# A two-block transformer kernel: mid-kernel loads issued by GpSimd, latent keys at 288 columns, memory squares added by VectorE, head sums in three steps

## What is computed

```python
kv_a = hk @ w_kv_a                                  # 1024 x (256 + 32)
c_kv, k_rope = jnp.split(kv_a, [KV_LORA_RANK], axis=-1)
mem_n = rms_norm_2(mem, mem_norm[l])                # needs the mean of mem * mem
o = rms_norm_2(o, subln) * (1.0 - lam_init)         # differential heads, 128 channels each
y_br = y_br * silu(gate);  y = concat(y_br, y_mem * silu(g_mem)) @ w_out
```

## Time and profile before

| | |
|---|---|
| median of 3 runs | 1167.52 us (1166.16 to 1168.13) |
| the profiled execution, its own time | 1172.58 us |
| its span, first to last instruction | 1170.7 us |
| mean granted TensorE clock | 0.979 of full speed |
| PE busy | 1122.1 us, 96% of the span |
| DVE, ACT, POOL busy | 470.7, 284.9, 53.7 us |
| DMA | 195.67 MB, mean 167 GB/s |

### The profile page before, as it was taken

One profiled execution on the slowest core, in us unless ns is written; L12 is line 12 of the kernel. 1 busy time (PEld: TensorE's weight loads), 2 busy tenths in 40 slices (PEclk: granted clock), 3 DMA queues, 4 the chain that ended last, 5 costly groups with the idle time before them and its releaser, 6 DMA issues.

```text
span 1170.7 us, 19356 instructions
## 1 busy us (share of the span) xinstructions
PE 1122.1 (96%) x8435; PEld 945.8 (81%) x8435; DVE 470.7 (40%) x947; ACT 284.9 (24%) x680; POOL 53.7 (5%) x70
## 2 busy tenths in 40 slices
PE   6888999999999999899999999999999999999997
PEld 4657888888887858588888888888899888887676
DVE  8886445434314518713000000234834541602621
ACT  4622510000002444612000000133303241202632
POOL 3110011111100000000000000000003000000000
PEclk7998999999999999999999999999999999999999
DMA  9985879999843344073544532453440003544220
GB/s 285 341 278 188 287 267 373 335 352 361 317 149 116 108 126 146 14 238 109 180 143 146 178 108 81 143 157 118 126 145 4 4 3 108 180 149 139 73 72 36
DMA packets 122019, 195.67 MB, mean 167 GB/s; under 512 B 5796, under 2 KB 104782, under 8 KB 115534
## 3 DMA queue, kind: packets, MB, share of 16 engines
q1 hardware_dynamic: 110778, 131.15, 35.0%
q0 software_dynamic: 9360, 59.77, 13.2%
q10 hardware_dynamic: 1796, 3.50, 1.0%
HBM read 191.53 MB, written 1.05 MB: 164 GB/s over the span
## 4 chain that ended last, share of the span: by engine, by line
PE 83%; DVE 10%; ACT 3%; issue 1%; DMA 1%; SPq 0%; ACTq 0%; DVEq 0%
PE psum L658 63%; PE psum L1029 13%; DVE arena L1717 3%; ACT arena L2562 2%; PE psum L933 2%; PE psum L1504 1%; DVE sq L1717 1%; DVE arena L1723 1%; DMA arena<-in_x 1%; ACT sq L2562 1%; DVE xT L1723 1%; PE psum L1479 1%; DVE arena L1981 1%; DVE arena L1720 1%; PE psum L1626 1%
## 5 line engine op out<-in xcount | busy, mean ns | idle before, releaser
L658 PE MATMUL psum<-hT,ring 128*128 128x256 f32 x1392 | 311.4, 381 | 1.7 <-DVE hT L1723 0.8
L658 PEld LDWEIGHTS psum<-hT,ring 128*128 128x128 f32 x1392 | 263.1, 191 | 41.0 <-issue 6.0
L2562 ACT ACTIVATE arena<-psum 128x256 f32<-128x256 f32 (+5 forms) x219 | 98.0, 475 | 649.1 <-PE psum L658 597.6
L658 PE MATMUL psum<-hT,arena 128*128 128x256 f32 (+1 forms) x960 | 165.2, 346 | 3.4 <-DVE hT L1717 3.4
L658 PEld LDWEIGHTS psum<-hT,arena 128*128 128x128 f32 (+1 forms) x960 | 143.9, 186 | 22.6 <-issue 4.5
L1717 DVE TENSOR_TENSOR arena<-arena,psum 128x256 f32<-128x256 f32 (+2 forms) x76 | 39.2, 530 | 264.2 <-ACT arena L2562 235.6
L658 PE MATMUL psum<-arena 64*64 64x64 f32 (+6 forms) x2156 | 108.0, 240 | 0.9 <-ACT arena L2562 0.5
L658 PEld LDWEIGHTS psum<-arena 64*64 64x64 f32 (+3 forms) x2156 | 91.0, 141 | 12.4 <-issue 8.6
L1029 PE MATMUL psum<-arena,ring 128*128 128x256 f32 x384 | 85.1, 380 | 0.0
L1029 PEld LDWEIGHTS psum<-arena,ring 128*128 128x128 f32 x384 | 72.6, 190 | 11.0 <-issue 1.2
L658 PE MATMUL psum<-ring,arena 128*128 128x256 f32 (+2 forms) x288 | 73.2, 415 | 0.5 <-ACT arena L2562 0.5
(11 more groups left out here) (259 smaller groups left out, 1112.8 us busy)
## 6 DMA issues: line engine op xcount, KB each, us to landing
aring<-in_ada_w POOLq DMA_DIRECT2D x36, 1024.0 KB, 8.5
ring<-in_a_w_in SPq DMA_DIRECT2D x14, 1024.0 KB, 5.4
arena<-in_ffn_w_gate SPq DMA_DIRECT2D x12, 1024.0 KB, 7.5
arena<-in_ffn_w_up SPq DMA_DIRECT2D x12, 1024.0 KB, 8.0
ring<-in_ffn_w_down SPq DMA_DIRECT2D x12, 1024.0 KB, 5.0
ring<-in_ffn_w_gate SPq DMA_DIRECT2D x10, 1024.0 KB, 9.4
ring<-in_ffn_w_up SPq DMA_DIRECT2D x10, 1024.0 KB, 7.6
arena<-in_ffn_w_down SPq DMA_DIRECT2D x10, 1024.0 KB, 5.0
```

The costliest lines, as they stand in the source:

```text
L658: return eng.matmul(dst, w, x, start=first, stop=last)
L2562: return eng.activation(dst, x, f, **k)
```

## The change

Five edits, none of which changes what is computed:

1. The 12 loads leave ACT's list and go to POOL's, each behind a wait for a point at which its destination is free: `("dn", 0, 3)` emptied, `q1_mean`, `("dn", 1, 3)` emptied, and `post_added`.
2. `w_kv_a` is split by rows (7 and 1 chunks k) instead of by columns; PE makes one pass of 288 columns.
3. The memory squares are taken by ACT in four pieces and added by DVE (`sum_squares`, behind `ada_bias(7)`); PE makes one matmul with ones, between `cqt` b = 0 and b = 1. ACT's root of it moves from ahead of part 4 to ahead of part 5.
4. RWKV: `scale_tokens(0, i)` goes into the last chunk, `memory_gate(0)` ahead of the last gain.
5. Last layer: head sums at u = 2, 3, 4 (four matmuls each); DVE copies the bank to SBUF at u = 4 and ACT takes the root of the copy; SiLU at 7, 8, 8; `gate_heads` ahead of memory step 11.

The diff, its core (indents shortened):

```diff
 pair_sum = stat[:, :].rearrange("p (m t) -> p m t", t=T)[:, 0:4:3, :]
 square_sum = stat[:, 0:T]
 root_cols, rstd_cols = stat[:, T:T + 2], stat[:, T + 4:T + 6]
-SUMS = [("ms", 1), ("ms", 2), ("ms", 3), ("ms", 4), ("ms_out", 0), ("ms", 5)]
+SUMS = [("ms", 1), ("ms", 2), "ms_mem", ("ms", 3), ("ms", 4), ("ms_out", 0), ("ms", 5)]
 COLUMN_NORMS = [("ms", 1), ("ms", 2), ("ms_out", 0)]
...
-SUM_STEP, SCALE_STEP, ROW_STEP = 4, 9, 10
-SILU_STEPS = [7, 8, 9]
+SUM_STEPS, SCALE_STEP, ROW_STEP = [2, 3, 4], 9, 10
+SILU_STEPS = [7, 8, 8]
...
 in_columns(("glu",), a["s5_w_glu"][0], D)
 swiglu_weights(0)
 w_kva = a["w_kv_a"].rearrange("(k p) n -> p k n", p=P)
-weights.append((w_kva[:, :, 0:RKV], (KC, RKV), ("kva", 1)))
-weights.append((w_kva[:, :, RKV:], (KC, DR), ("kva", 1)))
+KVA_SPLIT = KC - 1
+for ks in (slice(0, KVA_SPLIT), slice(KVA_SPLIT, KC)):
+    weights.append((w_kva[:, ks, :], (ks.stop - ks.start, RKV + DR), ("kva", 1)))
 weights.append((a["mla_w_dq"][0].rearrange("(k p) n -> p k n", p=P), (KC, RQ), ("cqt", 1)))
...
@@ -961,18 +962,9 @@
-    def mean_square(key, chunks, src, sig, count, pool="a"):
+    def mean_of_sum(key, pool="a"):
         eng.wait_ge(*next_bank(key, pool))
-        ps = bank_of(key)
-        for k in range(chunks):
-            eng.wait_ge(done(sig), count(k))
-            last = mm(ps[:, 0:T], ones, src[:, k, :], k == 0, k == chunks - 1)
-        last.then_inc(*fills(key))
-
-    def mean_of_sum(key):
-
-        eng.wait_ge(*next_bank(key))
         eng.wait_ge(done("square_sums"), SUMS.index(key) + 1)
         mm(bank_of(key)[:, 0:T], ones, square_sum).then_inc(*fills(key))
@@ -1153,26 +1145,24 @@
...
     ada_rows(7, "b")
     for b in range(2):
         eng.wait_ge(*next_bank(("kva", b)))
-    w, landed = panel()
-    eng.wait_ge(*landed)
+    kva_w = [panel() for _ in range(2)]
+    eng.wait_ge(*kva_w[0][1])
     for b in range(2):
         ps = bank_of(("kva", b))
         for k in range(KC):
             if b == 0:
                 eng.wait_ge(done("h_ready"), KC + k + 1)
-            mm(ps[:, 0:RKV], hT3[:, k, b * P:(b + 1) * P], w[:, k, :], k == 0, k == KC - 1)
+                if k == KVA_SPLIT:
+                    eng.wait_ge(*kva_w[1][1])
+            w = kva_w[0][0][:, k, :] if k < KVA_SPLIT else kva_w[1][0][:, k - KVA_SPLIT, :]
+            last = mm(ps[:, 0:RKV + DR], hT3[:, k, b * P:(b + 1) * P], w, k == 0, k == KC - 1)
+        last.then_inc(*fills(("kva", b)))
+    row_columns(7, row_late, "b")
     w, landed = panel()
     eng.wait_ge(*landed)
     for b in range(2):
-        ps = bank_of(("kva", b))
-        for k in range(KC):
-            last = mm(ps[:, RKV:RKV + DR], hT3[:, k, b * P:(b + 1) * P], w[:, k, :], k == 0, k == KC - 1)
-        last.then_inc(*fills(("kva", b)))
-    row_columns(7, row_late, "b")
-    mean_square("ms_mem", KC, mem_sq, "mem_squares", lambda k: 1, "b")
-    w, landed = panel()
-    eng.wait_ge(*landed)
-    for b in range(2):
+        if b:
+            mean_of_sum("ms_mem", "b")
         eng.wait_ge(*next_bank(("cqt", b)))
         ps = bank_of(("cqt", b))
         for k in range(KC):
@@ -1566,15 +1556,17 @@
         if m == 2 * KC - 1:
             last.then_inc(*fills(("b_in", i)))
-    def head_sums():
-
...
-        eng.wait_ge(*next_bank("sub"))
+    def head_sums(i):
+
+        if i == 0:
+            eng.wait_ge(*next_bank("sub"))
         ps = bank_of("sub")
-        for h in range(HB):
-            eng.wait_ge(done("o_squares"), h // 2 + 1)
+        eng.wait_ge(done("o_squares"), i + 1)
+        for h in (2 * i, 2 * i + 1):
             for b in range(2):
                 last = mm(ps[:, b * HB + h:b * HB + h + 1], o_sq[:, h, b * P:(b + 1) * P], ones[:, 0:1])
-        last.then_inc(*fills("sub"))
+        if i == 2:
+            last.then_inc(*fills("sub"))
     def head_scales():
...
         else:
-            if u == SUM_STEP:
-                head_sums()
+            if u in SUM_STEPS:
+                head_sums(SUM_STEPS.index(u))
             if u == SCALE_STEP:
                 head_scales()
...
         .then_inc(*v.signals("rotary_angles"))
     ada_bias(7)
+    sum_squares("mem_squares", 0, (1, 2, 3), mem_sq)
     inverse_root("ms_mem")
...
+    def scale_tokens(b, i):
+
+        key, three = ("rstd7", b, i), slice(3 * i, 3 * i + 3)
+        eng.wait_ge(*filled_at(key))
+        x = yT7[:, three, b * P:(b + 1) * P]
+        tt(x, x, bank_of(key)[:, 0:3 * P].rearrange("p (m t) -> p m t", t=P), ALU.mult).then_inc(*v.empties(key))
+
...
             gated_gain(range(NBR))
         else:
             gain_chunk(c - 1)
+        if c == NCR - 1:
+            eng.wait_ge(*v.last)
+            for i in range(2):
+                scale_tokens(0, i)
         if c < NCR - 1:
...
-    def scale_tokens(b, i):
-
-        key, three = ("rstd7", b, i), slice(3 * i, 3 * i + 3)
-        eng.wait_ge(*filled_at(key))
-        x = yT7[:, three, b * P:(b + 1) * P]
-        tt(x, x, bank_of(key)[:, 0:3 * P].rearrange("p (m t) -> p m t", t=P), ALU.mult).then_inc(*v.empties(key))
-
-    eng.wait_ge(*v.last)
-    for i in range(2):
-        scale_tokens(0, i)
+    memory_gate(0)
     gain_chunk(NCR - 1)
+    gained = v.last
     inverse_variance(1)
-    memory_gate(0)
-    eng.wait_ge(done("vector_step"), v.n)
+    eng.wait_ge(*gained)
     for i in range(2):
         scale_tokens(1, i)
         for pair in ((0,), (1, 2))[i]:
...
@@ -2527,12 +2522,16 @@
         else:
             if u >= SCALE_STEP:
                 scale_heads(u - SCALE_STEP)
+            if u == SCALE_STEP + 2:
+                for i in range(3):
+                    gate_heads(i)
             attend(memory(1), [u])
+            if u == SUM_STEPS[-1]:
+                eng.wait_ge(*filled_at("sub"))
+                V.tensor_copy(sub_rstd, bank_of("sub")[:, 0:2 * HB]).then_inc(*v.empties("sub"))
             if u == SCALE_STEP - 2:
-                eng.wait_ge(*emptied_at("sub"))
+                eng.wait_ge(done("sub_root"), 1)
                 V.reciprocal(sub_rstd, sub_root).then_inc(*v.signals("sub_rstd"))
-    for i in range(3):
-        gate_heads(i)
     eng.wait_ge(done("gate_ready"), 4)
     memory_gate(1)
...
@@ -2811,13 +2810,6 @@
     take_memory(0)
     take_memory(1)
-    eng.dma_start(pos_i.bitcast(I32), a["positions"][0].rearrange("(b p) -> p b", p=P),
-                  allow_slow_non_contiguous=True)\
-       .then_inc(done("positions_landed"), 16)
-    for m, names in enumerate((("k_nope_norm_g", "k_rope_norm_g"), ("mla_q_nope_norm_g", "mla_q_rope_norm_g"))):
-        for name, lo, hi in zip(names, (0, DN), (DN, DQK)):
-            x = a[name] if m == 0 else a[name][0]
-            eng.dma_start(gain_rows[:, m, lo:hi], x.partition_broadcast(P)).then_inc(done("gain_rows_landed"), 16)
     root_columns(("ms", 2))
...
-    act(flat(mem_sq), flat(memT), ACT.Square).then_inc(*s.signals("mem_squares"))
+    for pair in range(4):
+        two = slice(2 * pair, 2 * pair + 2)
+        act(flat(mem_sq[:, two, :]), flat(memT[:, two, :]), ACT.Square).then_inc(*s.signals("mem_squares"))
...
     eng.wait_ge(*filled_at(("ms", 2)))
     parts = [(("kva", b), 0, RKV, b) for b in range(2)] + [(("kva", b), RKV, RKV + DR, 2 + b) for b in range(2)]
     parts += [(("cqt", b), 0, RQ, 4 + b) for b in range(2)]
     for key, lo, hi, i in parts:
-        if i == 4:
+        if i == 5:
             root("ms_mem")
         eng.wait_ge(*filled_at(key))
...
     act(flat(k_mem[1]), bank_of(("k_mem", 1, 0)), ACT.Copy, scale=HD ** -0.5).then_inc(*s.empties(("k_mem", 1, 0)))
-    for x, at in ((qh, CONST_HIDDEN), (kh, CONST_HIDDEN + T)):
-        eng.dma_start(x[DQK:DQK + 2], constants[0:2, at:at + T].unsqueeze(1).to_broadcast([2, H1, T]))\
-           .then_inc(done("hidden_landed"), 16)
     for b in range(2):
...
     squares(3)
-    for r, x in ((0, "a_w2_2"), (64, "a_a2_2")):
-        eng.dma_start(w2a2[r:r + 64, :], a[x][0]).then_inc(done("w2_landed"), 16)
-    eng.dma_start(masks7, constants[:, CONST_MASK:CONST_ALIBI]).then_inc(done("masks7_landed"), 16)
     root(("ms", 4))
...
         act(sq[:, two], xT[:, two], ACT.Square).then_inc(*s.signals("squares"))
-    eng.dma_start(alibi, constants[:, CONST_ALIBI:].rearrange("p (h b t) -> p h b t", b=2, t=T))\
-       .then_inc(done("alibi_landed"), 16)
-    eng.dma_start(post_gain, a["post_norm_2"][1].partition_broadcast(P)).then_inc(done("post_gain_landed"), 16)
     root(("ms", 5))
...
                 eng.wait_ge(*emptied_at(("do", 4 * u + 3)))
                 act(flat(o_sq[:, two, :]), flat(mixT[1][:, two, :]), ACT.Square).then_inc(*s.signals("o_squares"))
             if MEMORY_STEPS[u] == ("scores", MEMORY_PAIRS - 1):
-                eng.wait_ge(*filled_at("sub"))
-                act(sub_root, bank_of("sub")[:, 0:2 * HB], ACT.Sqrt, bias=eps_column, scale=1.0 / P)\
-                    .then_inc(*s.empties("sub"))
-            if u in SILU_STEPS:
-                gate_pair(SILU_STEPS.index(u))
+                eng.wait_ge(*emptied_at("sub"))
```

(28 more changed lines are left out.)

## The result

The changed kernel took **1152.78 us** (median of 4 runs, 1149.53 to 1153.47) beside 1166.84 us (4 runs) for the kernel before: ratio 0.9874, 95% interval 0.9851 to 0.9896. Run twice more it took 1154.82 us (5 runs, ratio 0.9887, interval 0.9864 to 0.9910) and 1153.97 us (4 runs, 0.9881, 0.9861 to 0.9902). All 13 runs have the median 1153.8. Beside them the kernel before had medians between 1166.8 and 1167.8. Taking their middle, 1167.4, the gain is 13.6 us (1167.4 - 1153.8), where 12.2 us was forecast.

The account below looks back on a forecast made before the run. PE was taken as the bound (83% of the chain). Work 9.0 plus clock 1.5 and 1.7 gave 12.2 us off the profiled 1172.58, thus 1160.4; less 5.06 to the median, 1155.3 us, range 1152.3 to 1160.0.

Parts of the forecast that it names:

- loads off ACT: Before the spread in the latent stage: ACT's root no longer waits behind load issues, so PE idles 1.2 us less.
- memory squares: Latent stage: eight matmuls with ones become one, saving 3.0 us at full clock, while DVE does the additions.
- RWKV end: After the last token variance: PE no longer waits 0.99 us for DVE's memory gate, saving 1.0 us.
- gates: End of last layer: PE no longer waits 1.09 us for gate_heads before the last projection, saving 1.1 us.
- clock behind latents: The half-clock stretch from 392.0 to 395.4 was expected to vanish with the narrow pass, saving 1.5 us.
- clock behind step 4: Last layer: half clock to 1119.1 was expected to vanish once the one-column head sums are split in three, saving 1.7 us.
- rival B: The fall at 378.4, behind the spread, goes as well and nothing is late: 13.7 us gained, 1153.8 us; chance 0.22.
- two thin slacks: Latent stage: DVE's additions finish 0.4 us before PE asks; normed memory for memory_kv(0) has 0.5 us to spare.
- rival C: DVE's sum or reciprocal makes PE wait up to 0.5 us each, or 288 columns cost 1.6 more: 1156 to 1158; chance 0.12.
- rival D: Positions loaded through POOL land too late, DVE's in-order list stalls PE; slower from a landing of some 24 us; chance 0.04.
- third fall: Half clock at 378.4, behind the idle time before the spread; worth another 1.5 us but left out of the sum.
- Rival A: Clock falls stay or come back elsewhere, so only the 9.0 us of work are gained: 1158.5 us; chance 0.20.

## Why the prediction was off

| term | forecast | measured |
|---|---|---|
| loads off ACT | 1.2 | 0.9 (4.44 - 3.53, both at full clock); 1.1 with the loads back alone |
| one pass | 2.7 | 2.68 |
| memory squares | 3.0 | 3.02 |
| RWKV end | 1.0 | 1.13 (2.49 - 1.36) |
| gates | 1.1 | 1.28 |
| sums fill waits | none | 0.44 |
| clock behind latents | 1.5 | 3 in 4 times 1.65 = 1.2 |
| clock behind step 4 | 1.7 | 4 in 5 times 1.36 = 1.1 |
| clock around the spread | none (rival B) | 5 in 6 times 1.56, less 2 in 13 times 1.0 = 1.1 (1.0 with 4 in 6, the falls behind the idle time) |
| clock at the RWKV end | none | 4 in 5 times 1.54 = 1.2 (one of the four lasted twice as long and cost 2.99) |
| sum | 12.2 | 9.5 + 4.7 = 14.2 (before rounding) |

The prices of the falls come from distances: 1.56 is the 24.64 of one pass alone, less 25.75 - 2.67; 1.65 is the rest of 28.96 - 25.75; 1.54 is 33.37 - 31.83 (one pass alone); 1.0 is 4.51 - 3.53.

**The work** was right to 0.5 us: 9.5 against 9.0. The two thin slacks held: DVE's last addition ended at 384.97, 0.4 us before PE asked, as worked out, so rival C's misses did not come.

**Loads on POOL.** The issue of the positions began at 368.72, and they landed in 3.0 us (3.3 before), some 7 us ahead of their use at 378.38; rival D is out. The first issue, under which DVE added two chunks from SBUF (368.34 to 369.02), took 0.72 us, the four behind it 0.54 to 0.56. By the Trainium skill, "SBUF — State Buffer", section "SBUF: two separate sides", GpSimd can be locked out of the port that it shares with DVE; here that could be 0.2 us at most. All 13 profiles with these loads on POOL have the same addition beside the first issue, so none shows whether it is the cause; their landings took 2.6 to 3.1 us.

**The step that failed** is the sentence "the column sums and transposes there remain, and I leave it to a rival": the third fall belonged in the sum. It was a term of the clock that was too small, 3.2 against 4.7 by the counts (and 6.8 us of half clock against 13 over all executions), in the direction of rival B. The two falls that were in the sum were worth 2.3, not 3.2, and two that weren't in it another 2.4. That the median of all runs is rival B's 1153.8 is therefore partly luck. The reason behind it was poor too. From one profile I took each fall as certain where I saw one and as absent where I saw none. The falls that I counted came in 3 of 4 and 4 of 5 profiles, and a fourth place, the RWKV end, didn't show in the one profile that I had.

Two smaller slips stand beside it. Rival B less a microsecond is 1152.8, not 1152.3, so the range was given half a microsecond too wide at its lower end. And an issue was priced at 0.45 us, while one of the five took 1.57; the 1.2 for the group was read from the rows and is not touched by that.

**Rival A** (the falls stay, 9.0 us) is out by the total. The page "TensorE: Matmul & The Clock Gate" of the Trainium skill, Part 1, puts falls down to idle time; the trace disagrees behind step 4 (busy 3.40 of 3.40, then 0.50) and agrees at the RWKV end, in one profile with the wait filled. The same page says that the gate's timing isn't tied to the kernel's start, so that one kernel is slowed differently from run to run; the 20 profiles agree.

**Open.** The terms give 14.2 and the medians 13.6. The stretch from `memory_kv(0)` to the last token variance, 559.2 to 559.8 us in the four profiles of the kernels before and 559.1 to 561.3 in the 16 others (559.6 and 560.0 on average), may hold the rest; I haven't traced it. Why the falls behind the narrow pass and step 4 come was not isolated, and whether they come as often as in the profiles isn't shown. Of the groups of loads moved later in the kernel, none was tried alone.

## What to carry to other kernels

Price removed work and waits from the rows, and check them as distances between instructions of PE, which repeated to 0.01 us here in most of the short stretches, while totals scattered by 2. Take a low-clock stretch in a profile as one draw: look at a second and third profile before it goes into a sum at full price or at none, and compare the mean granted clock over all executions. At the four places of this kernel where a short idle time or a stretch of tiny matmuls was removed, the counts put the clock at about a microsecond beside the work itself; elsewhere that is a guess. Look at each issue in a group of loads, too: here one of five was nearly the whole wait.

## What the runs showed of the hardware

The granted clock falls to the 1.2 GHz level for some 3.4 us in some executions of identical instructions and not in others: behind the untouched column sums of ms_out in 11 of 18 profiles, for 0.80 us of time (132.87 against 132.07). In some executions it also falls behind a stretch in which PE was busy without a break (3.40 of 3.40 us, then 0.50), most of it one-column matmuls. A matmul of 288 columns costs in proportion to one of 256 (7.83 / 16 = 0.49 us against 0.43), while the same columns as a pair of 256 and 32 take 0.65 (10.47 / 16, woven or in two passes): the narrow one adds 0.22 us where its columns add 0.06 in the wide one. In a group of five small loads on ACT's queue one issue took 1.26 to 1.67 us and the others 0.39 to 0.49, in seven of seven profiles; on POOL's queue, in 13 profiles, they took 0.54 to 0.72.
